# Scores and values of two pages in every second page step, with two buffers of turned keys and four page slots

## The reference, cut to what matters

```python
k_past = cache_k[a, page_table].reshape(b_s, past_len, N_HEADS, 2, HEAD_DIM)
v_past = cache_v[a, page_table].reshape(b_s, past_len, N_HEADS, V_DIM)
o_s = diff_attend(qs, pos_new, ((k_past, v_past, pos_past), (kn, vn, pos_new)), lam, slopes)
```

## Time and profile before

| | |
|---|---|
| median of 3 runs | 3104.95 us (3101.76 to 3109.3) |
| the profiled execution's own time | 3106.49 us |
| its span | 3104.7 us |
| PE / PEld / DVE / ACT / POOL busy | 98% / 94% / 48% / 34% / 9% of the span |
| transposes of keys (line 1904) | from 144.7 to 970.4 us of the span |
| granted clock of PE | 0.997 |

### The profile page before, as it was taken

One profiled execution on the slowest core, in us unless ns is written; L12 is line 12 of the kernel. 1 busy time (PEld: TensorE's weight loads), 2 busy tenths in 40 slices (PEclk: granted clock), 3 DMA queues, 4 the chain that ended last, 5 costly groups with the idle time before them and its releaser, 6 DMA issues.

```text
span 3104.7 us, 60197 instructions
## 1 busy us (share of the span) xinstructions
PE 3048.8 (98%) x25406; PEld 2915.5 (94%) x25406; DVE 1499.0 (48%) x2166; ACT 1061.5 (34%) x1502; POOL 292.2 (9%) x233
## 2 busy tenths in 40 slices
PE   8999999999988999999999999999999999999998
PEld 7988888888867999999999999998999999999998
DVE  4434444444455554444444444456444454445445
ACT  3234343434434433232322322235332323333333
POOL 0022222222200110000000000023000000000002
PEclk9999999999999999999999999999999999999999
DMA  6499999999998454444444444442444444444442
GB/s 198 155 357 381 371 378 376 380 371 371 372 370 298 136 166 149 139 146 136 147 139 149 136 149 136 149 137 90 149 150 149 149 149 150 149 150 149 150 150 88
DMA packets 378808, 638.05 MB, mean 206 GB/s; under 512 B 15624, under 2 KB 261871, under 8 KB 377999
## 3 DMA queue, kind: packets, MB, share of 16 engines
q1 hardware_dynamic: 373984, 620.68, 57.5%
q0 software_dynamic: 3328, 11.24, 1.1%
q10 hardware_dynamic: 1230, 2.29, 0.2%
HBM read 625.37 MB, written 9.23 MB: 204 GB/s over the span
## 4 chain that ended last, share of the span: by engine, by line
PE 93%; DVE 3%; ACT 2%; issue 1%; DMA 0%; POOL 0%; SPq 0%; ACTq 0%; DVEq 0%; POOLq 0%
PE ps L1793 74%; PE ps L1904 7%; PE ps L1928 4%; PE ps L1953 3%; DVE halves L1200 1%; ACT halves L883 1%; PE ps L2055 1%; PE ps L2211 1%; PE ps L2035 1%; DMA io_tm<-in_x_sample_dram 0%; PE ps L1942 0%; PE ps L1885 0%; DVE hid L1660 0%; PE ps L1989 0%; ACT keyT L958 0%
## 5 line engine op out<-in xcount | busy, mean ns | idle before, releaser
L1200 DVE TENSOR_TENSOR halves<-raw,halves 128x2048 fp32r<-128x2048 f32 x300 | 687.6, 2292 | 659.9 <-ACT halves L883 659.8
L883 ACT ACTIVATE halves<-raw 128x2048 fp32r<-128x2048 f32 x300 | 573.1, 1911 | 864.3 <-PE ps L1793 862.6
L1793 PE MATMUL ps<-yhi,halves 128*128 128x336 f32 x2816 | 650.1, 317 | 0.2 <-DVE halves L1200 0.2
L1793 PE MATMUL ps<-x1hi,halves 128*128 128x320 f32 x2816 | 622.0, 309 | 1.8 <-DVE halves L1200 1.8
L1793 PEld LDWEIGHTS ps<-yhi,halves 128*128 128x128 f32 x2816 | 477.5, 188 | 0.5 <-issue 0.5
L1793 PEld LDWEIGHTS ps<-x1hi,halves 128*128 128x128 f32 x2816 | 472.0, 188 | 2.1 <-issue 2.0
L1793 PE MATMUL ps<-ylo,halves 128*128 128x336 f32 x1408 | 440.7, 313 | 0.0
L1793 PE MATMUL ps<-x1lo,halves 128*128 128x320 f32 x1408 | 435.1, 309 | 0.0
L1793 PE MATMUL ps<-hA_hi,halves 128*128 128x336 f32 (+1 forms) x1408 | 377.7, 315 | 2.5 <-DVE hT L1684 2.5
L1793 PE MATMUL ps<-hB_hi,halves 128*128 128x336 f32 (+1 forms) x1408 | 375.8, 314 | 0.0
L958 ACT ACTIVATE keyT<-ps 128x512 f32<-128x512 f32 x256 | 153.1, 598 | 458.5 <-PE ps L1904 444.9
(11 more groups left out here) (234 smaller groups left out, 3670.5 us busy)
## 6 DMA issues: line engine op xcount, KB each, us to landing
raw<-in_w_gate_up_dram SPq DMA_DIRECT2D x176, 1024.0 KB, 5.1
raw<-in_cache_k_dram SPq DMA_DIRECT2D x200, 512.0 KB, 6.7
raw<-in_cache_v_dram SPq DMA_DIRECT2D x194, 512.0 KB, 7.2
raw<-in_w_down_dram SPq DMA_DIRECT2D x88, 1024.0 KB, 5.0
kv_raw<-in_w_qkv_dram SPq DMA_DIRECT2D x64, 512.0 KB, 7.7
page<-in_cache_v_dram SPq DMA_DIRECT2D x62, 512.0 KB, 7.2
page<-in_cache_k_dram SPq DMA_DIRECT2D x56, 512.0 KB, 6.9
raw<-in_w_qkv_dram SPq DMA_DIRECT2D x16, 1024.0 KB, 5.1
```

The source lines that it names most:

```text
L883: act.activation(whi[t][:, :], raw[r][:, :], ACT.Copy).then_inc(hi_ready[t], 1)
L1200: dve.tensor_tensor(wlo[t][:, :], raw[r][:, :], whi[t][:, :].bitcast(F32), ALU.subtract)\
L1793: mm = pe.matmul(out, l, r, start=first and n == 0, stop=last and n == 2)
```

## The change

Even steps no longer compute scores and values. Odd step t computes the scores of page t - 1, the values that the step before would have done, the scores of page t, and the values of this step, in this order. So that the turned keys of two pages can wait, `keyT` becomes two buffers; the second lies where the fifth page slot (`page4`) was, so the ring has 8 half slots instead of 10, and later 12 instead of 14. `PAGE_ORDER` stays as it is.

```diff
-SLOTS = 14
+SLOTS = 12
@@ page_slots
-    last, turns, out = {i: None for i in range(10)}, {i: 0 for i in range(SLOTS)}, []
+    last, turns, out = {i: None for i in range(2 * RAW)}, {i: 0 for i in range(SLOTS)}, []
...
-            last.update({i: None for i in range(10, SLOTS)})
+            last.update({i: None for i in range(2 * RAW, SLOTS)})
@@ trunk
-        page4 = place("page4", [P, UNIT], F32, z); z += UNIT * 4
+        keyT = [place("keyT1", [P, UNIT], F32, z)]; z += UNIT * 4
...
-        pages = [w[:, 1024 * half:1024 * half + 1024] for w in raw + [page4] + late for half in range(2)]
+        pages = [w[:, 1024 * half:1024 * half + 1024] for w in raw + late for half in range(2)]
...
-        keyT = place("keyT", [P, UNIT], F32, z); z += UNIT * 4
+        keyT = [place("keyT0", [P, UNIT], F32, z)] + keyT; z += UNIT * 4
@@ SP
-                    elif slot < 2 * RAW + 2:
-                        sp.wait_ge(unit_used[1], 9)
@@ keys_out, on ACT (and the same on DVE)
-                if t:
-                    act.wait_ge(s_full, t)
-                act.activation(keyT[:, 512 * g:512 * g + 512], ps[g % 2][:, :], ACT.Copy)\
+                if t > 1:
+                    act.wait_ge(s_full, t - 1)
+                act.activation(keyT[t % 2][:, 512 * g:512 * g + 512], ps[g % 2][:, :], ACT.Copy)\
@@ DVE, the loop over t
-                scores_out(t)
+                if t % 2:
+                    scores_out(t - 1)
+                    scores_out(t)
@@ PE, scores(t)
-                if 0 <= t - TURN_LAG < PAGES - GROUP:
-                    pe.wait_ge(pt_out, t - TURN_LAG + 1)
+                last = t + 1 - t % 2 - TURN_LAG
+                if 0 <= last < PAGES - GROUP:
+                    pe.wait_ge(pt_out, last + 1)
...
-                                   keyT[:, P * j:P * j + P], start=(a == 0), stop=(a == 3),
+                                   keyT[t % 2][:, P * j:P * j + P], start=(a == 0), stop=(a == 3),
@@ PE, turn_probs(v)
-                pe.wait_ge(s_out, min(v + TURN_LAG, PAGES))
+                pe.wait_ge(s_out, min(2 * ((v + TURN_LAG) // 2), PAGES))
@@ PE, the loop over t
-                scores(t)
-                for v in valued_in(t):
-                    values(v)
+                if t % 2:
+                    scores(t - 1)
+                    for v in valued_in(t - 1):
+                        values(v)
+                    scores(t)
+                    for v in valued_in(t):
+                        values(v)
```

More of the change, by code:

```diff
@@ L1392, in keys_out @@
                 dve.wait_ge(kt_full, 4 * t + g + 1)
-                if t:
-                    dve.wait_ge(s_full, t)
-                dve.tensor_scalar(keyT[:, 512 * g:512 * g + 512], ps[g % 2][:, :], 1.0, None, ALU.mult)\
+                if t > 1:
+                    dve.wait_ge(s_full, t - 1)
+                dve.tensor_scalar(keyT[t % 2][:, 512 * g:512 * g + 512], ps[g % 2][:, :], 1.0, None, ALU.mult)\
                     .then_inc(kt_dve, 1)
```

## The result

The changed kernel takes 3295.51 us (median of 4 runs, 3294.13 to 3303.68), the kernel before on the same chip 3107.12 us (4 runs, 3101.76 to 3115.42): 1.0618 times as long, 95% interval 1.06 to 1.0636. The forecast was 3148 us and its range ended at 3190; the sign was right, the size was not.

A forecast was written before the change was run, and what follows sets the result against it. PE was taken to set the pace, with the DMA engines nearly full. 53 pairs at 1.43 us stall less 0.51 gain make +49 us, the other 11 -6: +43 on the median 3104.95, so 3148 us, range 3098 to 3190.

The forecast's parts named there:

- the first landing: First load of a burst after the freed slot, from issue to landing: taken as 4.0 us, between 3.8 and 4.7.
- stall of the odd step: PE's wait for odd pages' keys: 0.7 us, or 2.0 with weights in front, 1.43 us a pair on average.
- A piece costs 0.524 MB / 399 GB/s = 1.31 us of all 16 engines: Service time of each 512 KB load queued ahead of the odd keys, at the highest DMA rate seen: 1.31 us.
- PE is busy for 659 of 660 us at full clock: PE in the stretch from 200 to 860 us before the change, read as PE setting the pace.
- Net gain 0.51 us a pair: Paired block on PE: 0.61 us of width-change pauses saved less 0.1 us of wait; 33 us over 64 pairs.
- the wait for DVE in the block: Second scores of a block wait for DVE to take the first out of `ps[2]`: some 0.1 us.
- The other 11 pairs: Pairs outside the 53, four before the ring first closes and seven late: -0.51 us each, -6 us together.
- A: Rival: the loads keep up, keys land by 7.1 us and only the gain stays, 3072 us; chance 0.10.
- B: Rival: shorter fixed transfer part in a burst, first landing 3.2 us, stall and gain nearly cancel, 3099 us; chance 0.11.
- C: Rival: first landing is the loaded queue's throughout, keys at 9.2 us, 2.1 us stall in every pair, 3184 us; chance 0.14.
- The two "issue" waits halved: Sign in the profile: PE's "issue" waits before key transposes and scores, 200 to 860 us, halved in number.
- The rate: Sign in the profile: DMA rate of the stretch from 200 to 860 us down from 376 to about 351 GB/s.

The follow-up runs named there:

- e9: Kernel before with four page slots, scores in every step, but values of two pages done together in the odd step: 3297.12 us, 1.0626.
- e3: Changed kernel with only SP's load order changed: keys of both pages of a pair in front of its values, weights behind those keys: 3116.57 us, 1.0049.
- e10: Changed kernel, SP reading each odd key page's number (9 to 113) three more times, so those key loads are issued later: 3301.44 us, 1.0628.
- e11: Changed kernel, SP reading each odd key page's number before it waits for the values' slot, so the keys are issued earlier: 3298.32 us, 1.0631.
- e1: Changed kernel with 20 unread transposes of the identity in front of each odd step's key transposes, pages 9 to 115: 3271.96 us, 1.0554.
- e6: e3 with the weight piece of an even step issued between the two key pages instead of after them: 3116.18 us, 1.0046.
- e7: e3 with both the edits of e5 and e6: 3120.76 us, 1.005.
- e2: Kernel before with four page slots instead of five, nothing else of the change: 3109.29 us, 1.0016.
- e5: e3 with both pages' values placed between the two scores of the odd step's block: 3122.78 us, 1.0066.

## Why the prediction was wrong

Right were the mechanism and its place: keys of odd pages behind values whose slot frees once in two steps (e9 has the loss with that alone, e3 loses it by the order alone). Right also were the issue after the freed slot (0.94 predicted, 0.95 measured, mean of 53 bursts), the first landing (4.0, and 4.29), the time at which PE wants the keys (7.1, and 7.2), and that the load engines are then not full. Terms of the sum were mis-sized. In us, means of the 53 pairs from 9 to 113, added up from the trace's single records, each rounded:

| term | predicted | changed kernel |
|---|---|---|
| first values to landing of the odd keys | 8.54 | 9.86 |
| stall of the odd step | 1.43 | 2.67 |
| even step | 4.46 | 4.05 |
| odd step with the block | 8.09 | 9.77 |
| pair | 13.98 | 16.50 |

**The pieces ahead of the keys.** This is the step that failed first: "A piece costs 0.524 MB / 399 GB/s = 1.31 us of all 16 engines". That rate is one of a queue that is never empty. In a burst after an idle queue a piece takes about 1.8 us: (8.94 - 0.97 - 4.45)/2 = 1.76 in the 23 bursts without weights, (10.56 - 0.94 - 4.16)/3 = 1.82 in the 30 with. The prediction had seen that the queue would be nearly empty, and priced only the first landing by it. Most of the excess is the second piece, which lands 1.95 us behind the first in the 23 bursts and 2.24 in the 30; those behind it come some 1.6 us apart. With the first landing's 0.29, for which the earlier trace rows had the right size in its median of 4.3 and not in its shortest 3.8, that makes the 1.24 us more of stall, 66 us over 53 pairs; the 0.24 us for stores is not counted apart. Why a burst starts that slowly (249 GB/s from 550 to 556 us) is open; it is not the moment at which SP issues the keys (e10, e11).

**The clock, claimed at nothing.** "PE is busy for 659 of 660 us at full clock" was read from the stage as it was; the prediction itself put a wait into every pair and did not ask what the clock does then. The row at 560 us shows it at its lower level after a wait. e3's odd and even steps, at full clock and without a stall, take 9.03 + 4.01 = 13.04 us, the changed kernel's 9.77 + 4.05 = 13.82: 0.78 us, 41 us over 53 pairs. The two kernels differ in the order of their loads, so this is an estimate; e1, which brings the clock back, gains 0.63 us a pair by its steps and 24 us by its time. The Trainium skill has the rule that applies ("TensorE: Matmul & The Clock Gate", Part 1: an array that idles falls to half its clock); this trace agrees (0.50 behind the wait that ended at 559.39), and the prediction should have weighed it as soon as it had found a wait.

**The gain.** 13.04 us in e3 against 12.55 predicted for a pair without a stall: "Net gain 0.51 us a pair" was nothing on average (before takes 13.02). The two pauses were counted at the full length that they have in the row of the weight loads, and the wait for DVE in the block, priced at 0.1 us, is 0.27. In pairs without other waits 0.24 to 0.29 us is there, and others lose as much. In e3 the waits of turned blocks for DVE (line 1887: 5.7 us, 7 times in 660) and four longer "issue" waits of the transposes (1.1 to 1.4 us, 0.4 at most before; PE's row puts such waits down to ACT's copies of keys) stand in odd steps, behind the short even ones; e6 and e7 removed neither. The eleven pairs that hold them are 11 of the 12 that became over 0.59 us longer than before. That without them the gain would be whole was not shown. This term is 26 us over 53 pairs. The waits of e3 from 200 to 860 us:

```profile
PEld ps L1906 <- issue: 23.4, 54, 1.4
...
PEld ps L1887 <- DVE kTh L1330: 5.7, 7, 1.1
...
PE ps L1906 <- ACT keyT L958: 3.8, 5, 1.1
```

**The rest.** Of the 190 us between the two profiled executions 184 lie in the 53 pairs, 53 x (16.50 - 13.02). The other 11 pairs cost under 1 us (1.4 more ahead of the 53, 0.8 less behind them) instead of bringing 6. Some 5 us stand outside the page steps, where both kernels do the same; e2's profiled execution differs there from the kernel before by more. Together 11.

66 + 41 + 26 + 11 = 144 of the 147 us by which the forecast was short.

**The rivals.** A and B are out: PE waits for loads, and long. B's first landing of 3.2 us stands against 4.29 measured. The Trainium skill's price ("DMA: Bandwidth & Descriptors", "Anatomy of one DMA") makes the same estimate of 3.2 us; the measurement decides. In A, the landing below which the sign turns is about 2.9 us and not 3.1: the prediction's own terms leave pairs without weights no wait below 3.3, and a wait can't be less than nothing. C came nearest in its number, keys at 9.2 us, but by a wrong reason: no loaded queue, the first landing was that of an idle one, and the flight of 6.7 us from the keys' own issue is 5.27 us where they are issued later (e10). Nor did any of the three have the clock in it, so even C's 3184 was 110 us short.

**What would have shown it.** Wait in front of odd pages about 53 times: yes, in 52 pairs, but 142 us (53 x 2.67) and not 76. The two "issue" waits halved: those of the transposes a step yes, those of the scores no, since the wait for DVE stands there now. The rate: 300 GB/s and not 351.

## What to carry to other kernels

Ask of every regrouping of work how often it frees the slots of a ring, and what stands behind the freed slot in the issuing queue: a load that waits for a late slot also holds back loads whose own slot is long free, and an order that put these first took the whole wait away here (e3). Price a burst by rows of bursts, and by their median, not by the rate of a full queue. And where a forecast puts waits into an engine that had none, reprice the work behind them at the lower clock.

## What the runs showed of the hardware

- Loads of 512 KB after an idle queue: the first lands 4.29 us after its issue (mean of 53 bursts), the second 1.95 to 2.24 us behind it, further ones some 1.6 us apart, where a full queue moves one in 1.31 us (399 GB/s).
- Waits of the array of 2.5 us on average, up to 5.7, once in 16.5 us, brought the granted clock of the stage from 1.00 to 0.93; eight transposes behind one took 1.57 us instead of 0.85.
- A pause in the row of the weight loads is mostly no time of the kernel: from e3 to e5 the pauses of a block, its leaving included, shrank by 0.33 us (0.27 + 0.41 to 0.15 + 0.20), the block by 0.02.
